# A two-layer hybrid encoder trunk: the gated linear attention's output made token-major, and the activations moved 32 bytes

## What is computed

```python
for l in range(DEPTH):
    x = x + 0.5 * swiglu(rmsnorm(x, ffn1_norm[l]), ...)        # d_ff = 2816
    x = x + hybrid_mixer(rmsnorm(x, mix_norm[l]), w_in[l], ..., w_out[l])
    x = x + 0.5 * swiglu(rmsnorm(x, ffn2_norm[l]), ...)
return rmsnorm(x, final_norm)

def hybrid_mixer(h, ...):
    q_a, k_a, v_a, q_g, k_g, v_g, gate_lr, r_g = jnp.split(h @ w_in, ...)
    attn = rmsnorm(sliding_window_attention(q_a, k_a, v_a, sinks), attn_out_norm)
    o = gla_chunked(q_g, k_g, v_g, log_a)     # 4 heads of 128 columns, chunks of 64 tokens
    gla = rmsnorm(o, gla_out_norm) * silu(r_g)    # the norm is over each head's 128 columns
    return concat([attn, gla]) @ w_out
```

## Time and profile before

| | |
|---|---|
| timed runs | 936.21, 936.03 and 930.25 us; median 936.03 us |
| the profiled execution's own time | 929.8 us |
| its span, first to last instruction | 928.2 us |
| PE busy, PEld busy | 99%, 98% of the span |
| DVE busy, ACT busy | 65%, 49% |
| mean granted clock of TensorE | 0.998 of full speed |
| DMA | 169.06 MB, mean 182 GB/s |

### The profile page before, as it was taken

The page is one execution under the profiler, slowest core; times in us unless marked ns, Lnnn a source line. Parts: engine busy times, 40 slices in busy tenths (PEclk is TensorE's granted clock), DMA queues, the critical chain, the costliest instruction groups (busy, mean ns, idle before and its releaser), DMA issues.

```text
span 928.2 us, 19280 instructions
## 1 busy us (share of the span) xinstructions
PE 920.3 (99%) x8130; PEld 913.3 (98%) x8130; DVE 607.1 (65%) x701; ACT 454.8 (49%) x498; POOL 3.5 (0%) x7
## 2 busy tenths in 40 slices
PE   9999999999999999999999999999999999999997
PEld 9999999999999999999999999999999999999996
DVE  7765565688768665555686655567796785565554
ACT  7444444457746444444554344446675644444443
POOL 0000000000000000000000000000000000000001
PEclk9999999999999999999999999999999999999999
DMA  8675655563246655655556555655613665655531
GB/s 284 235 233 189 210 181 193 178 204 108 75 163 220 224 183 185 202 193 188 181 196 218 183 184 188 214 182 143 223 47 92 227 227 184 213 191 181 199 118 46
DMA packets 130997, 169.06 MB, mean 182 GB/s; under 512 B 3344, under 2 KB 116752, under 8 KB 130960
## 3 DMA queue, kind: packets, MB, share of 16 engines
q1 hardware_dynamic: 130384, 167.86, 54.9%
q10 hardware_dynamic: 576, 0.66, 0.2%
HBM read 167.46 MB, written 1.05 MB: 182 GB/s over the span
## 4 chain that ended last, share of the span: by engine, by line
PE 96%; DVE 1%; DMA 1%; ACT 1%; SPq 0%; issue 0%; POOLq 0%; DVEq 0%
PE ps L380 30%; PE ps L382 30%; PE ps L381 30%; PE ps L630 1%; PE ps L643 1%; DMA raw<-in_ffn_w_down 1%; DMA resid<-in_xt 1%; DVE wlo L1137 1%; PE ps L468 0%; PE ps L767 0%; PE ps L790 0%; PE ps L777 0%; DVE xlo L1126 0%; PE ps L725 0%; PE ps L702 0%
## 5 line engine op out<-in xcount | busy, mean ns | idle before, releaser
L1121 DVE TENSOR_TENSOR wlo<-raw,whi 128x2048 fp32r<-128x2048 f32 x157 | 351.3, 2238 | 237.4 <-ACT whi L863 237.4
L380 PE MATMUL ps<-xhi,whi 128*128 128x256 f32 x1648 | 457.6, 278 | 0.0
L381 PE MATMUL ps<-xlo,whi 128*128 128x256 f32 x1648 | 455.2, 276 | 0.0
L382 PE MATMUL ps<-xhi,wlo 128*128 128x256 f32 x1648 | 455.2, 276 | 0.0
L863 ACT ACTIVATE whi<-raw 128x2048 fp32r<-128x2048 f32 (+2 forms) x158 | 295.8, 1873 | 145.1 <-PE ps L382 141.9
L380 PEld LDWEIGHTS ps<-xhi,whi 128*128 128x128 f32 x1648 | 309.4, 188 | 1.8 <-issue 1.0
L381 PEld LDWEIGHTS ps<-xlo,whi 128*128 128x128 f32 x1648 | 309.5, 188 | 0.0
L382 PEld LDWEIGHTS ps<-xhi,wlo 128*128 128x128 f32 x1648 | 309.5, 188 | 0.0
L380 PE MATMUL ps<-h_parts,whi 128*128 128x256 f32 x768 | 212.4, 277 | 0.1
L381 PE MATMUL ps<-h_parts,whi 128*128 128x256 f32 x768 | 212.1, 276 | 0.0
L382 PE MATMUL ps<-h_parts,wlo 128*128 128x256 f32 x768 | 212.1, 276 | 0.0
(11 more groups left out here) (168 smaller groups left out, 500.4 us busy)
## 6 DMA issues: line engine op xcount, KB each, us to landing
raw<-in_ffn_w_down SPq DMA_DIRECT2D x44, 1024.0 KB, 4.7
raw<-in_ffn_w_gate SPq DMA_DIRECT2D x42, 1024.0 KB, 5.2
raw<-in_ffn_w_up SPq DMA_DIRECT2D x42, 1024.0 KB, 5.2
raw<-in_w_in SPq DMA_DIRECT2D x12, 1024.0 KB, 5.0
raw<-in_w_in SPq DMA_DIRECT2D x8, 512.0 KB, 4.3
raw<-in_w_out SPq DMA_DIRECT2D x8, 512.0 KB, 4.3
raw<-in_w_in SPq DMA_DIRECT2D x2, 1088.0 KB, 5.1
raw<-in_w_out SPq DMA_DIRECT2D x8, 256.0 KB, 3.8
```

Source lines behind the costliest of these rows:

```text
L380: pe.matmul(o, w_hi, x_hi, start=start, stop=False, skip_group_check=True)
L381: pe.matmul(o, w_hi, x_lo, start=False, stop=False, skip_group_check=True)
L382: return pe.matmul(o, w_lo, x_hi, start=False, stop=stop, skip_group_check=True)
L1121: nc.vector.tensor_tensor(lo, r, h.bitcast(F32), ALU.subtract).then_inc(lo_done, 1)
```

## The change

In words:

- `M_R0` and `M_R1` go through `project_tokens`, so that the gate is token-major in PSUM. ACT takes its silu straight from there, scaled by the token's norm factor (`gate_out`). DVE's two multiplications of the gate go.
- The products that make o have their operands exchanged, so that o is token-major. Its intra-chunk part keeps its shapes. In the products with the states, 64 columns of `qe` now stand still and 128 columns of `Sta` move; before, 128 columns of `Sta` stood still and 64 of `qe` moved.
- In token-major form a head's sum of squares lies along the row. ACT squares o from PSUM and sums in the same instruction, eight times into `osum`. The copy of o and `gla_sums` on PE go.
- DVE multiplies o by its token's factor and the gate in eight instructions of 128 columns; PE transposes the eight pieces behind the second unit of `w_out` (L805 of the changed kernel); ACT and DVE take `xhi` and `xlo` from PSUM with the gain as factor.
- The eight spreads behind that unit stay (`SETTLE = 8`), behind the transposes, and nothing reads what they write.
- PE waits for `sg_done` before `M_R1`, where it waited for `rg_ev`, and for `og_done` before the transposes, where it waited for `o_ev`.
- `rs_gap` becomes `osum` with the same size and `gap_x` grows by 8 floats. Everything behind it moves by 32 bytes: `xhi` and `xlo` from 448 to 480, and `h_parts` from 192 to 224 bytes past a multiple of 512, where the weights start.

The diff, cut to its core:

```diff
+SETTLE = 8
-        sb("rs_gap", [P, 8])
-        sb("gap_x", [P, 96])
+        osum = sb("osum", [P, 8])
+        sb("gap_x", [P, 104])
@@ PE
-                project(M_R0, t, tiles(0), attention_sums)
+                project_tokens(M_R0, t, [ps[0][:, 0:UC], ps[0][:, UC:2 * UC]], attention_sums)
...
-                for h in range(GH):
-                    j = h // 2
-                    for tt in range(TT):
-                        pe.matmul(o_tile(h)[:, tt * P:(tt + 1) * P], vg[:, tt, h * P:(h + 1) * P],
-                                  AT[:, 4 * (h % 2) + 2 * j + tt, :],
+                for tt in range(TT):
+                    for h in range(GH):
+                        pe.matmul(o_tile(tt, h), AT[:, 4 * (h % 2) + 2 * (h // 2) + tt, :], vg[:, tt, h * P:(h + 1) * P],
...
-                            last = pe.matmul(o_tile(h)[:, c * CHUNK:(c + 1) * CHUNK], Sta[b:b + DK, c - 1, j, :],
-                                             qe[b:b + DK, j, c * CHUNK:(c + 1) * CHUNK],
+                        last = pe.matmul(o_tile(c // 2, h)[r:r + CHUNK, :], qe[b:b + DK, j, c * CHUNK:(c + 1) * CHUNK],
+                                         Sta[b:b + DK, c - 1, j, :], start=False, stop=True, skip_group_check=True)
...
-                pe.wait_ge(rg_ev, 2 * l + 1)
-                project(M_R1, t, tiles(0), gla_sums)
+                pe.wait_ge(sg_done, 4 * l + 2)
+                project_tokens(M_R1, t, [ps[0][:, 0:UC], ps[0][:, UC:2 * UC]])
...
-                        pe.wait_ge(o_ev, 2 * ev)
-                        spread([ps[1], ps[2]], 5 * l + 3, rs_y, 8).then_inc(rG_ps, 1)
+                        pe.wait_ge(og_done, 2 * ev)
+                        for h in range(GH):
+                            for tt in range(TT):
+                                last = pe.transpose(ps[3 * (h // 2)][:, (h % 2 * TT + tt) * P:(h % 2 * TT + tt + 1) * P],
+                                                    o_tok[:, tt, h * P:(h + 1) * P], ident)
+                            if h % 2:
+                                last.then_inc(og_ps, 1)
+                        spread([ps[1], ps[2]], 5 * l + 3, rs_y, SETTLE)
@@ ACT
+                def gate_out(i):
+                    act.wait_ge(unit_done, ST + 3 * t + i + 1)
+                    c = UC * (i == M_R1)
+                    for tt in range(TT):
+                        nc.scalar.activation(sg_tok[:, tt, c:c + UC], ps[0][:, tt * UC:(tt + 1) * UC], ACT.Silu,
+                                             scale=rcol[:, tt:tt + 1]).then_inc(sg_done, 1)
+                gate_out(M_R0)
                 split_mix(10)
...
+                            e = nc.scalar.activation(o_sq[:, tt, h * P:(h + 1) * P], o_tile(tt, h), ACT.Square,
+                                                     accum_out=osum[:, GH * tt + h:GH * tt + h + 1])
+                gate_out(M_R1)
                 split_mix(11)
@@ DVE
-                nc.vector.tensor_tensor(sg[:, 0:2, :], tiles(0), r_tiles(2), ALU.mult).then_inc(rg_ev, 1)
...
-                nc.vector.tensor_scalar(rs_v[:, :], ps[3][:, 0:8], EPS * P, None, ALU.add).then_inc(eps_in, 1)
+                nc.vector.tensor_scalar(rs_v[:, :], osum[:, :], EPS * P, None, ALU.add).then_inc(eps_in, 1)
...
+                        e = nc.vector.scalar_tensor_tensor(out=o_tok[:, tt, c], in0=o_tile(tt, h),
+                                                           scalar=rs_y[:, GH * tt + h:GH * tt + h + 1],
+                                                           in1=sg_tok[:, tt, c], op0=ALU.mult, op1=ALU.mult)
+                    e.then_inc(og_done, 1)
                 split_mix(11)
```

More of the change, by code:

```diff
@@ L783, in gla_sums @@
[L783 to L793, removed]
@@ L795, in mix @@
-                pe.wait_ge(rg_ev, 2 * l + 1)
-                project(M_R1, t, tiles(0), gla_sums)
+                for c in range(1, NCH):
+                    for h in range(GH):
+                        j, b, r = h // 2, DK * (h % 2), CHUNK * (c % 2)
+                        last = pe.matmul(o_tile(c // 2, h)[r:r + CHUNK, :], qe[b:b + DK, j, c * CHUNK:(c + 1) * CHUNK],
+                                         Sta[b:b + DK, c - 1, j, :], start=False, stop=True, skip_group_check=True)
+                        if c == NCH - 1 and h >= 2:
+                            last.then_inc(o_ps, 1)
@@ L1017, in mix @@
                 nc.scalar.activation(unread[:, :], ones[:, 0:2], ACT.Silu).then_inc(table_in, 1)
-                def mixed_hi(dst, src):
-                    nc.scalar.activation(dst, src, ACT.Copy).then_inc(mhi_done, 1)
+                def gate_out(i):
[5 more added lines that the diff above has]
+                gate_out(M_R0)
                 split_mix(10)
-                act.wait_ge(rg_ev, 2 * l + 1)
-                nc.scalar.activation(sg[:, 0:2, :], sg[:, 0:2, :], ACT.Silu).then_inc(sg_done, 1)
                 for b in range(2):
[L1026 to L1034, removed]
+                    act.wait_ge(am_done, 2 * l + b + 1)
+                    nc.scalar.activation(at_parts[:, 0, 2 * b:2 * b + 2, :], at32[:, 2 * b:2 * b + 2, :], ACT.Copy
+                                         ).then_inc(mhi_done, 1)
+                for p in range(2):
+                    act.wait_ge(o_ps, 2 * l + p + 1)
+                    for h in (p, p + 2):
+                        for tt in range(TT):
+                            e = nc.scalar.activation(o_sq[:, tt, h * P:(h + 1) * P], o_tile(tt, h), ACT.Square,
+                                                     accum_out=osum[:, GH * tt + h:GH * tt + h + 1])
+                    e.then_inc(osq_done, 1)
+                gate_out(M_R1)
                 split_mix(11)
-                act.wait_ge(rg_ev, 2 * ev)
-                nc.scalar.activation(sg[:, 2:4, :], sg[:, 2:4, :], ACT.Silu).then_inc(sg_done, 1)
                 split_mix(12)
@@ L1040, in mix @@
                 for b in range(2):
-                    act.wait_ge(am_done, 4 * l + b + 3)
-                    mixed_hi(xhi[:, 4 + 2 * b:6 + 2 * b, :], o32[:, 2 * b:2 * b + 2, :])
+                    act.wait_ge(og_ps, 2 * l + b + 1)
+                    nc.scalar.activation(xhi[:, 4 + 2 * b:6 + 2 * b, :], tiles(3 * b), ACT.Copy,
+                                         scale=par[:, G_GLA:G_GLA + 1]).then_inc(mhi_done, 1)
                 split_mix(14)
@@ L1446, in mix @@
                 dve.wait_ge(eps_in, ev)
                 rsqrt(5 * l + 3, rs_v[:, :], 8, P, rs_y[:, 0:8])
-                done(M_R1)
-                nc.vector.tensor_tensor(sg[:, 2:4, :], tiles(0), r_tiles(2), ALU.mult).then_inc(rg_ev, 1)
-                split_mix(11)
[L1451 to L1456, removed]
+                dve.wait_ge(rs_step, RS * (5 * l + 4))
@@ new lines, in mix @@
+                dve.wait_ge(sg_done, 4 * ev)
+                for tt in range(TT):
+                    for h in range(GH):
+                        c = slice(h * P, (h + 1) * P)
+                        e = nc.vector.scalar_tensor_tensor(out=o_tok[:, tt, c], in0=o_tile(tt, h),
+                                                           scalar=rs_y[:, GH * tt + h:GH * tt + h + 1],
+                                                           in1=sg_tok[:, tt, c], op0=ALU.mult, op1=ALU.mult)
+                    e.then_inc(og_done, 1)
@@ L1457, in mix @@
+                split_mix(11)
                 split_mix(12)
-                dve.wait_ge(og_done, ev)
-                dve.wait_ge(rG_ps, ev)
                 for b in range(2):
[L1461 to L1465, removed]
+                    dve.wait_ge(mhi_done, 4 * l + b + 3)
+                    for f in range(2):
+                        m = 4 + 2 * b + f
+                        e = nc.vector.scalar_tensor_tensor(out=xlo[:, m, :], in0=tiles(3 * b)[:, f, :],
+                                                           scalar=par[:, G_GLA:G_GLA + 1],
+                                                           in1=xhi[:, m, :].bitcast(F32), op0=ALU.mult, op1=ALU.subtract)
+                    e.then_inc(mlo_done, 1)
```

34 lines of the change are left out of this document (13 added, 21 removed).

## The result

The changed kernel takes 960.86 us (median of four runs, 960.59 to 961.29). The kernel before, timed with it, takes 933.14 (929.79 to 936.21). The ratio is 1.0298, with a 95% interval of 1.025 to 1.0346: slower, and outside the range of 921 to 941 us. The profiled execution took 960.89 us, its span is 958.9 us.

What follows compares the result with a forecast made beforehand. PE alone, busy 99%, was taken as the bound. Per layer -1.8 + 0.8 + 0.3 - 0.3 = -1.0 us, -2.0 for both: 929.8 to 927.8, plus 0.5 for timed runs, about 928.5 us; range 921 to 941.

Steps and rivals of the forecast that it cites:

- What bounds the kernel: Whole kernel: PE alone sets the time, by its matmul count and pace, 113.2 or 117.7 ns, kept until an interruption.
- a slow long stretch: Feed-forward step: about 1,464 uninterrupted matmuls at the second pace would take 6.6 us more.
- The work on PE: Mixer of each layer: PE work shrinks by 1.0 us, 2.0 for both layers; by the bounds 1.0 to 3.0.
- the states' products: 24 rows in each mixer, 1.48 us before: between 0 and -0.46 us, taken as -0.3.
- the eight transposes: New on PE beside the spreads in each mixer: loss 0.8 us, at most 0.9.
- The token-major term: `M_R0` and `M_R1`, 96 matmuls at 117.7 ns: loss 0.32 or 0.22 us by layer, taken as 0.3.
- What must stay hidden: ACT and DVE work in the mixer: PE waits for none; covers 2.1 us at the transposes, 1.4 at the third `w_out` unit.
- The rival with a late chain: `og_done` or the split behind it late: squares at 0.6 us, not 0.39, shrink the gain to 1.4 us; chance 0.04.
- The 32 bytes: Moved `xhi`, `xlo` and `h_parts`, read by every large matmul: effect on the pace taken as 0.
- The bound above: Worst pace change from the new offset, per large matmul: the second pace, +4.5 ns.
- The slower rival: Streams fall to the second pace as a rule: 6.6 us each feed-forward step, 948 us at three, 954 at four; chance 0.12.
- The clock: Sixteen transposes in a row could drop PE's clock to 1.2 GHz: 11 us for two layers, 939 us; chance 0.02.

Runs made afterwards that it cites:

- b_all_spreads: The kernel before with eight unread spreads behind the pair of spreads ahead of each of the four long feed-forward stretches; 959.44 us.
- b_new_offsets: The kernel before with only the padding changed (`gap_x` from 96 to 104), so `xhi` and `xlo` at 480, `h_parts` at 224; 963.68 us.
- b_all_moved: The kernel before with 32 bytes of padding in front of the weights, so activations move but keep their distances from the weights; 936.36 us.
- a_spreads_first: The changed kernel at the old offsets (`gap_x` 96), with the eight unread spreads ahead of the eight transposes instead of behind them; 934.13 us.

## Why the prediction failed

- *What bounds the kernel* held: PE alone, and its pace beside its work. The reading that a stream has one of two paces and keeps it until an interruption held at distance 192, but for the pauses in the first stretch, where no foreign matmul stands. The estimate of 6.6 us for a slow long stretch held: the last one takes 172.4 us in b_all_spreads and 165.9 in the kernel before. The timed runs differ by such steps; none of the slower runs of the kernel before has a trace. Over all sessions 50 runs of the kernel before were timed: 23 near 929.9 us, 24 near 936.3, two at 943.4, one at 949.6, and none between.
- *The work on PE* was forecast as -1.0 us for each layer, -2.0 together. At the same offsets it measured -2.8 (b_new_offsets against the changed kernel). The terms: the states' products 1.02 us where 1.48 stood, so the bound of -0.46 and not the -0.3 taken; the eight transposes 0.87 us, as bounded. The token-major term has the other sign at the new offsets, 96 x (116.7 - 118.3) = -0.15 us for each layer instead of +0.3. With these, -1.8 + 0.87 - 0.46 - 0.15 = -1.5 for each layer, -3.1 in all. The traces bear it out: from the start of `M_V0` to the first matmul behind the transposes it is 37.07 us in the changed kernel and 38.56 in b_new_offsets.
- *What must stay hidden* stayed so. The covers were forecast as 2.1 and 1.4 us; measured, `og_done` comes 270.94 - 268.58 = 2.4 us early. A square with its sum takes 0.25 us and not 0.39. The rival with a late chain didn't occur.
- *The 32 bytes* is the step that failed. I took 0 for the pace and gave its loss 0.12. It cost 33.8 us alone. The bound above was too low as well: it stood at +4.5 ns, the second pace, and the new offset gave 118.3 - 113.3 = +5.0, in the short streams too. The slower rival named the mechanism in part (a pace near the second, as a rule, 954 us for four steps). But in it the streams would have fallen to the known second pace. They got another one, and the two paces were gone altogether: the changed kernel's times lie within 0.7 us.
- The reasoning ahead of that 0 was weak at a point that the rows could have shown. Equal paces at 448 and 192 said that 256 bytes make no difference, nothing more. The exchange of operands turned a distance of 192 into one of 64 modulo 256, and cost 4.5 ns. That was a row with another distance, and it spoke for a loss. I used it as a sign that addresses matter and then weighed it at nothing.
- The Trainium skill states two independent read ports and says that loading the next weights takes no read bandwidth from the running matmul ("TensorE: Matmul & The Clock Gate", Step-by-step: what each phase is for). The conclusion drawn from it, that the shift is worth 0, doesn't hold here: the same matmuls at the same clock take 113.3 to 120.1 ns with the distance of the two operands. Whether the two reads disturb each other, or something else does it, no run shows.
- *The clock* stayed at its upper level (9 in all slices) through sixteen transposes in a row, so that rival is out.

Two things were new to me beside it. The order of the change has a loss of its own, some 20 us at the old offsets, that stands in no sum of instructions. And it doesn't show in the changed kernel, where at the new offsets neither of the two paces appears.

What stays open: why the distance of 192 modulo 256 is the one with the fast pace, and what decides which of its two paces a stream takes. The traces show the steps, not what is behind them. Distances between multiples of eight bytes weren't tried.

## What to carry to other kernels

Where PE bounds a kernel of float32 matmuls with 256 moving columns, measure the pace in nanoseconds from start to start for each pair of operands before counting instructions, and take any edit that moves a tensor, even an unnamed padding, for an edit of every matmul that reads it. The pace followed the distance between moving and standing operand, and neighbours of the best distance were among the worst, so try the distances on the chip. If the times of one kernel fall into steps, look for long streams that run at one of two paces, and for what interrupts PE ahead of them, a short pause included.

## What the runs showed of the hardware

- With 128 standing and 256 moving float32 columns, at the upper clock, a matmul starts each 113.3 to 120.1 ns, by the distance of the operands modulo 256 bytes. In long stretches 192 gives 113.3 or 117.8; 184 and 200 give about 120.
- The distance counts from standing to moving operand, with its sign: exchanged operands have the pace of the same distance (32: 116.7, 96: 120.0, 224: 118.2), and that of 32 isn't that of 224.
- Moving all of them together by 32 bytes changes nothing (b_all_moved: 936.36 us).
- At 192 a stream of up to some 1,500 matmuls keeps one of two paces through the units, a switch of the moving operand included. It can change behind foreign matmuls, and it changed at a pause of 0.28 us instead of 0.11 between two starts (a_spreads_first). The order alone of eight spreads and eight transposes is worth 15.5 us (949.61 against 934.13).
